# Host-tiled weights, a transposed copy of x, two 1024-token halves and rolling accumulation fronts in an eight-core decoder layer

## The reference, cut to what matters

```python
D_MODEL = 2048; BATCH = 8; SEQ = 2048; FFN_HIDDEN = 5632; HEAD_DIM = 128
DILATED_GROUPS = ((128, 1), (512, 4), (2048, 16))   # 8 heads in each group
def reference(x, w_in, conv_w, w_attn_o, w_conv_o, w_out, ln1_g, ln1_b,
              w_ffn_gate, w_ffn_up, w_ffn_down, ln2_g, ln2_b):
        proj = x @ w_in[layer]                      # (B, S, 19456)
        q, k, v, u, c_gate, b_gate, g_attn, g_conv = jnp.split(proj, split_points, axis=-1)
...
        for g, (window, dilation) in enumerate(DILATED_GROUPS):
            o_g, lse_g = dilated_band_attention(q[:, :, g], k[:, :, g], v[:, :, g], window, dilation)
...
        attn = attn.reshape(b, s, ATTN_OUT_WIDTH).astype(x.dtype) @ w_attn_o[layer]
        conv = (b_gate * causal_short_conv(c_gate * u, conv_w[layer])) @ w_conv_o[layer]
        merged = (jax.nn.sigmoid(g_attn) * attn + jax.nn.sigmoid(g_conv) * conv) @ w_out[layer]
        x = layer_norm(ALPHA * x + merged, ln1_g[layer], ln1_b[layer])
        hidden = jax.nn.silu(x @ w_ffn_gate[layer]) * (x @ w_ffn_up[layer])
        x = layer_norm(ALPHA * x + hidden @ w_ffn_down[layer], ln2_g[layer], ln2_b[layer])
```

## Time and profile before

| | |
|---|---|
| Time, median of 3 runs | 5203.41 us (5172.44 to 5708.37) |
| Profiled execution: span of its slowest core (core 1) | 5213.5 us; the cores lie between 5110.7 and 5213.5 us |
| PE busy | 4799.1 us, 92% of the span, 27912 matmuls |
| DVE, ACT, POOL busy | 1284.7, 573.4, 447.2 us |
| Mean granted TensorE clock of core 1 | 0.964 |
| Read from and written to HBM | 1073.78 MB and 79.69 MB |

### The profile page before, as it was taken

The page is one execution under the profiler, slowest core; times in us unless marked ns, Lnnn a source line. Parts: engine busy times, 40 slices in busy tenths (PEclk is TensorE's granted clock), DMA queues, the critical chain, the costliest instruction groups (busy, mean ns, idle before and its releaser), DMA issues.

```text
span 5213.5 us, 66518 instructions; the slowest of 8 cores (5110.7 to 5213.5 us)
## 1 busy us (share of the span) xinstructions
PE 4799.1 (92%) x27912; PEld 2436.9 (47%) x27912; DVE 1284.7 (25%) x1808; ACT 573.4 (11%) x833; POOL 447.2 (9%) x506
## 2 busy tenths in 40 slices
PE   5999999999899899999988889999899999988996
PEld 3566666666444444444443334444444444443442
DVE  1233332333421220034122000521310043122002
ACT  1111111111100110010111000100200010111000
POOL 1100101100000011100001111000111100001110
PEclk7999999999899999999999999999999999999998
DMA  5988878743555799977569999665899976579996
GB/s 81 107 101 102 101 94 98 94 47 48 154 150 152 124 140 147 164 165 204 152 135 115 129 149 163 183 173 158 110 144 157 154 178 193 153 121 122 145 161 107
DMA packets 1084228, 700.59 MB, mean 134 GB/s; under 512 B 159648, under 2 KB 1068960, under 8 KB 1073056
## 3 DMA queue, kind: packets, MB, share of 16 engines
q0 software_dynamic: 620800, 444.63, 65.5%
q1 hardware_dynamic: 463136, 251.72, 17.9%
HBM read 1073.78 MB, written 79.69 MB: 221 GB/s over the span
## 4 chain that ended last, share of the span: by engine, by line
PE 73%; DMA 19%; DVE 4%; issue 2%; ACT 1%; POOL 0%; DVEq 0%; POOLq 0%; ACTq 0%; SPq 0%
PE pb L330 72%; DMA slabs<-w_ffn_gate 12%; DMA slabs<-w_ffn_down 2%; DVE lnp L539 2%; DMA slabs<-wb_in 2%; DMA slabs<-w_ffn_up 1%; DMA xin<-x 1%; DVE small L611 1%; DMA slabs<-w_in 1%; PE pb L333 1%; DMA wb_in<-w_in 1%; DVE x1buf L339 0%; ACT arena L336 0%; ACT xin L336 0%; DVE x1buf L348 0%
## 5 line engine op out<-in xcount | busy, mean ns | idle before, releaser
L330 PE MATMUL pb<-arena,slabs 128*128 128x512 bf16 x14848 | 3306.6, 383 | 158.0 <-DMA slabs<-w_ffn_gate 76.7
L330 PEld LDWEIGHTS pb<-arena,slabs 128*128 128x128 bf16 x14848 | 1459.0, 99 | 1947.1 <-issue 283.4
L330 PE MATMUL pb<-slabs,arena 128*128 128x128 bf16 (+1 forms) x9984 | 1205.7, 283 | 31.6 <-DMA slabs<-w_ffn_down 18.6
L330 PEld LDWEIGHTS pb<-slabs,arena 128*128 128x128 bf16 x9984 | 738.4, 111 | 493.8 <-issue 46.5
L339 DVE TENSOR_TENSOR arena<-pb,tmps 128x512 bf16<-128x512 f32 x240 | 165.9, 691 | 1259.7 <-PE pb L330 1259.7
L336 ACT ACTIVATE tmps<-pb 128x512 f32<-128x512 f32 x368 | 218.2, 596 | 2189.7 <-PE pb L330 2189.6
L339 DVE TENSOR_TENSOR tmps<-pb,tmps 128x512 f32<-128x512 f32 x192 | 132.6, 691 | 849.5 <-PE pb L330 849.5
L109 POOL DMA_DIRECT2D slabs<-w_ffn_gate x88 | 100.5, 1143 | 2014.0 <-PE pb L330 1599.9
L348 DVE SCALAR_TENSOR_TENSOR x1buf<-x1buf,pb 128x512 f32<-128x512 f32 x128 | 83.7, 685 | 748.6 <-PE pb L330 748.6
L327 DVE CAST x1buf<-pb 128x512 bf16<-128x512 f32 x144 | 99.6, 692 | 668.2 <-PE pb L330 668.2
L330 PE MATMUL pb<-x1buf 128*128 128x128 bf16 x1200 | 171.1, 258 | 42.1 <-DVE x1buf L339 42.1
(11 more groups left out here) (47 smaller groups left out, 1003.2 us busy)
## 6 DMA issues: line engine op xcount, KB each, us to landing
slabs<-wb_in SPq DMA_DIRECT2D x160, 1024.0 KB, 7.1
slabs<-w_ffn_gate POOLq DMA_DIRECT2D x88, 1024.0 KB, 21.0
slabs<-w_ffn_up POOLq DMA_DIRECT2D x88, 1024.0 KB, 21.0
slabs<-w_ffn_down POOLq DMA_DIRECT2D x80, 1024.0 KB, 12.5
slabs<-w_in POOLq DMA_DIRECT2D x72, 512.0 KB, 12.4
slabs<-wb_co SPq DMA_DIRECT2D x32, 1024.0 KB, 6.2
slabs<-wb_o SPq DMA_DIRECT2D x32, 1024.0 KB, 6.5
wb_in<-w_in POOLq DMA_DIRECT2D x16, 1536.0 KB, 17.6
```

The costliest lines, as they stand in the source:

```text
L330: sch.op("pe", lambda e: e.matmul(out, lhsT, rhs, start=start, stop=stop), reads, writes)
```

## The change

The host lays every weight out as consecutive [128, 2048] float32 tiles of 1 MB, one contiguous 8 KB row per partition, and adds a transposed copy of x (`x_t`). On the chip nine slabs of 2048 bfloat16 elements per partition are filled from POOL, each by one casting DMA of one tile. The bfloat16 copies in HBM, the conversions and all PE transposes of x are gone (x for the first half is loaded once as `x_t` and stays through attention; that of the second half is loaded again). The transposes behind the first LayerNorm stay.

Projections run two head steps ahead instead of one (three slots of q, k, v), the last two head steps carry 12 steps each of the next stage, and `fin` is cut in four pieces of 512 columns. After attention there are two halves of 1024 tokens instead of four tiles of 512, and each slab feeds 32 matmuls in every stage, 504 slabs in all. w_out and w_ffn_down use `token_gemm`: up to four output blocks are open at once, each two matmuls further per slot, and a new one is begun every `gap` slots. The feed-forward is cut in three parts of 15, 15 and 14 of its 44 column blocks, each followed by its share of w_ffn_down, which is added to x1 in SBUF. The LayerNorm of a token block begins as its last piece of w_out or w_ffn_down is done, and its transposes stand between the matmuls of the later blocks.

```diff
-    NSLAB = 4
-    slabs = sb("slabs", [128, NSLAB, 4096], BF16)
+    NSLAB = 9
+    slabs = sb("slabs", [128, NSLAB, 2048], BF16)
+    class Slab:
+        def __init__(self, src):
+            self.gen = rr["slab"]
+            rr["slab"] += 1
+            self.i = self.gen % NSLAB
+            self.buf = B_slab[self.i]
+            self.view = slabs[:, self.i, :]
+            sch.dma("pool", S_slab[self.i], self.view, src, writes=[self.buf])
...
+    first_weights(0)
+    for tt in (0, 1):
+        for q in range(4):
+            load_xt(A0, 2048, tt, tt, q)
+    first_weights(1)
+    for tt in (2, 3):
+        for q in range(4):
+            load_xt(A0, 2048, tt, tt, q)
...
-            for qd in range(1):
+            for qd in range(4):
                 def fin(qd=qd):
-                    cs = slice(0, 2048)
+                    cs = slice(512 * qd, 512 * qd + 512)
...
+    def token_gemm(lhs, lhs_cells, nK, w_src, nslab, done, each_slot=None, R=4, c=2, pool=P_MAIN):
+        nch = (nK + c - 1) // c
+        gap = (nch + R - 1) // R
+        jobs = [(cb, tb) for cb in range(4) for tb in range(8)]
...
+        while nxt < len(jobs) or live:
+            if nxt < len(jobs) and len(live) < R and (not live or live[-1][1] >= gap):
+                live.append([jobs[nxt], 0, next_bank(pool)])
+                nxt += 1
+            for jb in list(live):
+                (cb, tb), k, (bk, bb) = jb
+                for kc in range(k * c, min(nK, k * c + c)):
+                    w, bw = wrow(cb, kc)
+                    mm(bk[:, :], lhs(kc, tb), w, kc == 0, kc == nK - 1, [bw] + lhs_cells(kc, tb), [bb])
+                jb[1] += 1
+                if jb[1] == nch:
+                    live.remove(jb)
+                    done(cb, tb, bk, bb)
+            if each_slot is not None:
+                each_slot()
...
+        def slot():                      # in out_proj: transposes of a block, four slots after it is done
+            for r in ready:
+                r[1] += 1
+            if ready and ready[0][1] >= 5:
+                transposes(ready.pop(0)[0])
...
+            def done(cb, tb, bk, bb, p=p):           # in ffn, after each output block of w_ffn_down
...
+                if p == 0:
+                    vstt(yv[:, cs], yv[:, cs], ALPHA, bk[:, :], ALU.mult, ALU.add, [bb] + cc, cc)
+                else:
+                    vtt(yv[:, cs], bk[:, :], yv[:, cs], ALU.add, [bb] + cc, cc)
+                if p == 2:
+                    ln_part(h, tb, cb)
+                    if cb == 3:
+                        ln_scalars(tb)
+                        if h == 1:
+                            ln_finish(h, tb, True)
```

More of the change, by code:

```diff
@@ new lines, in build_program, with attn_ap, make_head, weights @@
+    V_OFF = (RB + 28 * KB, RC + 8 * KB, RC + 12 * KB)
+    EPT_OFF = RB + 24 * KB
+    NUM, DEN = RC + 16 * KB, RC + 24 * KB
+    num, den = vf(NUM, 2048), vf(DEN, 2048)
+    c_num, c_den = cl(NUM, 8 * KB), cl(DEN, 8 * KB)
+    def attn_ap(h, t0, n):
+        half, o = divmod(t0, 1024)
+        off = RE + half * 16 * KB + h * 2 * KB + o * 2
+        return vb(off, n), cl(off, n * 2)
+    def make_head(i):
+        h, g = divmod(i, 3)
+        dil = GROUPS[g][1]
+        sl = i % 3
+        n_blk = 16 // dil
+        col = g * NHG + h
+        qT, kT = vb(Q_OFF(sl), 2048), vb(Q_OFF(sl) + 4 * KB, 2048)
+        cq, ck = cl(Q_OFF(sl), 4 * KB), cl(Q_OFF(sl) + 4 * KB, 4 * KB)
+        vsb = vb(V_OFF[sl], 2048).rearrange("p (b d) -> p b d", b=16)
+        cv = cl(V_OFF[sl], 4 * KB)
+        def weights():
+            if (i, "q") not in W0:
+                first_weights(i)
+        def proj_group(nm, dst, c_dst, tt):
+            weights()
+            sl_ = W0[(i, nm)]
+            wv = sl_.rows(16)
@@ L518, in issue_PV @@
                             src_ = tbk[:, :].rearrange("p (r i) -> p r i", r=4)
[L519 to L522 removed]
+                        vtt(dst, src_, dst, ALU.add, [tbb] + cA, cA)
         LOOK = 2
[L525 to L527 removed]
+        asteps = [lambda u=u: issue_S(u) for u in range(min(LOOK, nu))]
         for u in range(nu):
@@ new lines, in build_program @@
+    heads = [make_head(i) for i in range(24)]
+    for i, tts in ((0, (0, 1)), (1, (0, 1))):
+        pq, pk, pv = heads[i][:3]
+        if i == 0:
+            for tt in tts:
+                pq[tt](), pk[tt](), pv[tt]()
+        else:
+            for lst in (pq, pk, pv):
+                for tt in tts:
+                    lst[tt]()
+    for tt in (2, 3):
+        for i in (0, 1):
+            pq, pk, pv = heads[i][:3]
+            pq[tt](), pk[tt](), pv[tt]()
+    ucb0 = ucb_steps(0)
+    prev_fins = []
@@ L558, in build_program @@
+    for i in range(24):
+        A_, F_ = heads[i][3:]
+        if i + 2 < 24:
+            P_ = heads[i + 2][0] + heads[i + 2][1] + heads[i + 2][2]
+        else:
+            P_ = [ucb0.pop(0) for _ in range(12)]
         k = 0
@@ L793, in build_program @@
-    while pending_ln2:
-        pending_ln2.pop(0)()
+    gp["pool"] = P_ALL
+    for st in ucb0:
+        st()
+    for st in gate_steps(0):
+        st()
+    load_resid(0)
+    ffn(0, out_proj(0))
+    gp["pool"] = P_ALL
+    pend2 = [lambda tb=tb: ln_finish(0, tb, True) for tb in range(8)]
+    for n, st in enumerate(ucb_steps(1)):
+        st()
+        if n % 3 == 2 and pend2:
+            pend2.pop(0)()
+    for st in gate_steps(1):
+        st()
+    load_resid(1)
+    ffn(1, out_proj(1))
@@ L827 @@
+    for b in range(NCORES):
+        xt = x[b].T.reshape(16, 128, 4, 512).transpose(2, 1, 0, 3)
+        maps.append(dict(shared, x=np.ascontiguousarray(x[b]), x_t=np.ascontiguousarray(xt)))
+    return maps
 def kernel(**inputs):
```

816 lines of the change are left out of this document (369 added, 447 removed).

## The result

| | before | after |
|---|---|---|
| Median of the four paired runs | 5356.95 us | 5243.05 us |
| The single runs | 5172.44, 5203.41, 5510.49, 5708.37 | 4799.11, 4800.78, 5685.32, 5687.19 |
| Profiled execution, span of the slowest core | 5213.5 us (core 1) | 4799.2 us (core 4) |
| PE idle in it | 414 us | 151 us |
| Mean granted clock of that core | 0.964 | 0.991 |

The undisturbed runs compare as **0.925, interval 0.913 to 0.937**: the change makes the kernel faster. In the two longer runs of the kernel after, the cores of one die were granted less clock ("disturbed" from here on), and the median of four falls between the two kinds, which is why 5243 us stands so far from 4800. In both runs near 5686 us the cores of die 0 took 4793.1 to 4797.5 us at a clock of 0.991 or 0.992, and those of die 1 5663 to 5686 us at 0.816 to 0.821.

A forecast was written before the change was run, and what follows sets the result against it. PE was taken to bound the kernel: its own stream of 4696 us plus start 32, boundaries 18, handovers 10 and tail 64 gave 4820 us; with the median 0.2% under the span, the forecast was 4810 us, range 4740 to 4930.

The forecast's parts named there:

- The start: First two head steps: loading of weights and x adds 32 us beyond PE's work, bounds 20 and 65 us.
- Attention: Eight periods of three head steps at 147.35 us of PE work; reciprocal stalls priced 0, bound 42 us.
- Dense stages: After attention: 16128 matmuls with 512 columns at 217.2 ns each, 3503 us, bounds 216 to 218 ns.
- Slabs: Weight slab loads after attention: PE's waits for w_ffn_gate and x go to 0; bound +77 us.
- Rival (c): Its claim is not in the text given; counted among the slower outcomes, chance 0.04.
- Boundaries: First LayerNorm between w_out and feed-forward: PE idles 9 us per half, 18 us in all, bounds 0 and 52.
- Rival (a): Whole kernel: stalls move rather than vanish, in attention, boundaries, start and matmul rate; 4910 us, chance 0.17.
- Other handovers: Table loads and changes from one stage to the next cost 10 us.
- The tail: After PE's last matmul: eight token blocks of 9.4 us, partly beside PE, end 64 us later, bounds 50 and 75.
- The sum: Whole kernel: PE's stream plus start, boundaries, handovers and tail gives 4820 us against the span of 5213.5 us.
- rival (d): Whole kernel: the denser PE stream is granted less clock, 525 us more, 5335 us, slower; chance 0.07.
- The trace does not agree: Dense matmuls: rejected the skill's 13/16 clock rule and its 5904 us, citing clock 0.99 over 704 matmuls.

The follow-up runs named there:

- e7: The changed kernel with the reciprocal in one piece of 128x2048 instead of four pieces: 4844 to 4846 us undisturbed, ratio 0.941 to the kernel before.
- e4: The changed kernel with token_gemm holding one output block open at a time instead of up to four: 4857.72 and 4857.79 us undisturbed, ratio 0.927 to the kernel before.
- f11: The changed kernel with first loads reordered and the last LayerNorm spread over DVE, ACT and POOL: 4778 to 4781 us undisturbed, ratio 0.913 to the kernel before.
- f9: The kernel before with only the reciprocal cut in four pieces, one per attention piece: 5096 to 5140 us undisturbed, ratio 0.977 to the kernel before.
- f10: The kernel before with only the transposed copy of x, replacing block loads and transposes: 5222 to 5267 us undisturbed, ratio 1.004 to the kernel before.
- f12: The changed kernel with every input zero on all cores, same instructions, on the third chip: 4798 to 4800 us, ratio 0.916 to the kernel before.

## Why the prediction was right about the kernel and wrong about the median

**The start**, 32 us: right, 33 measured. The first two head steps were done at 119.4 us (forecast 118). The first matmul came at 19.3 us (16).

**Attention**, 8 x 147.35 us and no stalls: right, a period took 146.3 us, 8 us less in all. e7 confirms the price of the stall, 45 us against the bound of 42. PE waits 10.1 us in these periods all the same, for DVE in the line L272.

**Dense stages**, 217.2 ns: a little high. 697 matmuls in 150 us (core 0 of the kernel after, 3500 to 3650 us) are 215.2 ns; over 16128 this is 32 us less. This was the largest error of the sum.

**Slabs**, 0: right, none in the waits of PE. Rival (c) is out: casts were issued as close as 2.8 us apart and landed in 5.4 us, so several were in flight.

**Boundaries**, 18 us: mis-sized by half. The waits at the two of them are 28.7 us, 14 per half against the 9 that I took and the 5 to 12 that I named as a sign. Matmuls behind the waits run at a lower granted clock (0.91 over the window 2000 to 2080), which the term left out. That window holds 244 matmuls with 512 columns and 128 transposes, 60 us at 215.2 and 56 ns, so a boundary costs 20 us and both 41 us. Rival (a), with 26 us more, had this term right, and none of its other three. The mechanism, a front that drains to 12, 8 and 4 matmuls, is what the timeline shows, and e4 prices the fronts of w_out and w_ffn_down at 58 us.

**Other handovers**, 10 us: nothing of it came. The 10.1 us in the line L272 look like it and are not: they lie in the seven periods of attention, 1.4 us each, and are in the 146.3 us already. At changes of stage PE waits 0.2 us.

**The tail**, 64 us: right, 64.8 us from PE's last matmul to the end, 9.62 us per block for the 9.4 forecast.

**The sum**, 4820 against a span of 4799.2: 0.4% off, and the forecast of 4810 is 0.2% above the undisturbed runs. That it is so close is in part luck: 32 us of the dense stages, 8 of attention and 10 of handovers too much stand against 23 us too little at the boundaries.

**The step that failed** is the one from the sum to the median: "The median stood 0.2% under that span, so I forecast 4810 us." One of the three runs that I had been shown took 5708.37 us, and I treated it as something outside the sum: the lowered clock entered the forecast at nothing, and as rival (d) it got 0.07. It has since been met in 15 of 37 runs of the kernel after and its variants with real data, and in 19 of 43 of the kernel before. In the four runs here it came twice, at a mean clock of 0.816 to 0.821, and made the median 5243.05 us. With four runs of which each is disturbed with a chance of about 0.4, the median lies off the undisturbed time when two or more are, which is about one time in two. Against that chance no range of 190 us could hold.

Its price was wrong as well. I scaled 536 us, from a run which, by the windows of e4, may have been held for only a part of its length, to 525 us. A die held for nearly the whole run costs this kernel 886 to 928 us (5686 and 5727.54 against 4800), and the kernel before 704 to 733 us (5926.03 and 5954.67 against 5222). So where a die is held, the change is worth only about 4% (5686 / 5940 = 0.957, 5727.54 / 5940 = 0.964) instead of 7.5 to 8. That the old kernel loses less is argued, not shown: where PE waits for a transfer, a slower PE waits less.

I also wrote that **"The trace does not agree"** with the rule of the Trainium skill (page TensorE: Matmul & The Clock Gate, the warning on the peak-current limiter in Part 1), because 704 matmuls stood at 0.99. One profiled execution can't show that a clock is never lowered; the three times already did not fit it. The clocks of 0.811 to 0.821 are close to the 13/16 (0.8125) of that page, and 697 / 573 = 1.216 to its 16/13. In the level the traces agree with the page. The estimate of 5904 us by it was 3 to 4% too high against 5686 and 5727.54, and it came in some runs and not in others. By the wording of the rule it should have met every run of a chip with all eight cores in dense matmuls, taken the whole die and held as long as the load lasted. Here it met 4 runs in 10, and in both traces that show it (e4 and f11) it took a pair of cores at a time and let one pair go while its dense matmuls went on.

## What to carry to other kernels

Build the time of a new schedule from PE's own stream plus what is exposed around it: at 92% PE busy this gave the large terms within 1% and the total within half a percent, with errors of up to 32 us that partly cancelled. Then ask separately what the spread of the given times says: if one of three runs is 10% long, a median over four will be too in many cases, and it needs a chance and a price of its own, taken from the spread, before any range is written. For gate and up the layout of the weights in HBM was worth nothing once the bytes per matmul were halved, and an edit that seems local (the four reciprocal pieces, f9) can pay more than twice its own stall on the slowest core; why was not shown. And before a part of a change is judged by a variant (f10), look in the variant's waits for what the variant itself has added.

## What the runs showed of the hardware

- The granted clock can be held at 0.81 for nearly all of a run or a part of it: 573 instead of 697 matmuls with 512 columns in 150 us. In the two traces that show it, it held one pair of neighbouring cores (4 and 5, or 6 and 7) at a time or both, each pair over its own stretch (e4: 4 and 5 to about 3370 us, 6 and 7 from about 2160 us; f11: 6 and 7 to about 690 us, 4 and 5 from about 4310 us), while the other die kept its clock. In most disturbed runs only one die, either of the two, was met, in a few both.
- It met real data in about four runs of ten (15 of 37 and 19 of 43), and none of twelve runs with all inputs at zero, with the same instructions and transfers. If zeros had no effect and each run had a chance of 0.4, twelve in a row without one would have a chance of 0.6^12, or 0.2%; with the six of f12 alone, which ran where the new kernel with real data was met, it is 0.6^6, or 5%. What sets it off within a series of like runs stays open.
- A fused DVE operation over 128x2048 float32 (L293 of f11) took 2.35 us alone, or when it started first, and 4.1 us when one of POOL's additions of the same size was already running; those took 4.5 us alone and 6.55 us beside it.
- A DVE reciprocal over 128x2048 float32 took 12.95 us, one over 128x512 3.35 us (f9).
- A casting DMA that reads rows of 512 bytes landed 0.52 MB in 6.8 us in the median, one with 8 KB rows in 5.4 us.
- In the kernel before, the time that a core waits for the same slabs differed from 3.7 to 78.3 us between cores with the same program.
